# A decoder trunk's first microseconds: gain row fetched first on ScalarE's queue, first two weight units in pieces, rotary angles on GpSimd

## The chip, the cores and the metric

The kernel runs on one core of one Trainium2 chip. The metric is device time in microseconds (us) of one execution, lower is better, as the median of several runs. A core has TensorE (PE, matmuls and transposes), VectorE (DVE), ScalarE (ACT), GpSimd (POOL) and SyncE (SP, which only issues DMAs here). ScalarE and GpSimd also issue DMAs from their own queues.

## What is computed

Two decoder layers on 256 tokens of width 1024 in float32. Layer 0 mixes tokens by sliding-window attention with rotary positions, layer 1 by a gated delta rule. Each layer has two feed-forward blocks around the mixer:

```python
x = x + 0.5 * rmsnorm(swiglu(rmsnorm(x, norms[0]), w_in[0], w_out[0]), norms[1])
x = x + rmsnorm(mixer(rmsnorm(x, norms[2])), norms[3])
x = x + 0.5 * rmsnorm(swiglu(rmsnorm(x, norms[4]), w_in[1], w_out[1]), norms[5])

def swiglu(x, w_in, w_out):
    gate, up = jnp.split(x @ w_in, 2, axis=-1)
    return (jax.nn.silu(gate) * up) @ w_out

def rope_tables(positions, head_dim):
    ...
    ang = positions.astype(jnp.float32)[..., None] * inv_freq
    return jnp.cos(ang), jnp.sin(ang)
```

The hidden width of a feed-forward block is 2816. The rotary angles are 256 positions times 8 frequencies; they are used first in the attention of layer 0, which is the second of six stages.

## The kernel before

All matrix products are split: each float32 operand becomes a high part in the format fp32r (ScalarE copies it) and a low part (VectorE subtracts the high part from the original), and TensorE makes three products, high by high, weights' low by high, and weights' high by low. The weights of a stage come in **units** of 128 partitions x 2048 columns, 1 MB, through three slots of `w_raw`, each with its pair in `w_high` and `w_low`. SP issues a unit as two DMAs of 512 KB, and the fourth unit and all later ones wait until `w_lo` says that the low part of the unit three before is made (L284). ScalarE's `hi` makes the high part (L571, in the loop L577), VectorE's `lo` the low part (L1322).

The stages are ffn, swa, ffn, ffn, gdn, ffn. A feed-forward stage runs over 11 steps of 256 hidden columns; one step takes two units of `w_in` (four of the eight 128-row blocks of x each) and one of `w_out`. Each engine has its program written out by hand, in order, and steps 1 to 9 of a feed-forward stage are a hardware loop on each engine.

The start of the first stage (`enter(0)` on ScalarE and VectorE, `begin` and `first_tile` on TensorE) is what the change touches. Rows of x come in two tiles of 128 tokens, `t` = 0 and 1. VectorE multiplies each tile by the norm's weight row, in two halves of 512 columns (`x_gained`, L1394); the row, replicated over 128 partitions, is `gain_rows`, loaded by GpSimd's `gain_load` (L347). TensorE transposes each half (L855), and four **quarters** m = 0 to 3 of x turned stand in PSUM banks 6 and 7: ScalarE makes their high part (`turned`, L587), VectorE their low part (L1329). TensorE's first weight products (L844 to L846) are those of unit 0 with tile 0; then come the first half of unit 1, the transposes of quarter 2, the second half of unit 1 and the transposes of quarter 3, the last ones (`first_tile`). The norm's factor is not needed for that: it scales the products afterwards (`rstd`, from sums of squares of x by ScalarE, L621, and VectorE, L1420, and a power by GpSimd, L386 and L387), ahead of SiLU (L634).

After that VectorE runs `mul(0)`, `lo` of units 3 and 4, and `angles` (L1342 to L1364, the function of that name), once per launch; then its loop begins with the low part of the turned hidden units (`turn`, L1437), whose high part is ScalarE's (L639). TensorE's first product of `w_out` (L875) waits for it. The angles are reduced to the range of the sine; ScalarE computes sine and cosine from them after its loop of the first stage. GpSimd meanwhile loads the next gain rows and forms wide products for the next norm (`base_of_next`, L517 and L520).

The small constants (positions, sinks, decay parameters, convolution weights) are loaded by the first five instructions of ScalarE; two larger ones follow after the high part of unit 1 (L580, L581).

Of the kernel before, what the change touches and what calls it, by code (L numbers as in the profile page):

```python
# [34 lines left out]
P = 128  # L35
D = 1024
KT = D // P
TT = 2
# [46 lines left out]
def build(nc, x, positions, l0_norms, l0_ffn_w_in, l0_ffn_w_out, a_w_in, a_b_in, a_sinks, a_w_out,  # L85
# [4 lines left out]
    with ExitStack() as ctx:  # L90
# [72 lines left out]
        cwr = view(10752, P)  # L163

# [29 lines left out]
        raw_in = [sem(f"raw_in{s}") for s in range(SLOTS)]  # L194
        gain_in = [sem(f"gain_in{s}") for s in range(2)]
        w_hi, w_lo, w_used = sem("w_hi"), sem("w_lo"), sem("w_used")
        ident_built, tables = sem("ident_built"), sem("tables_built")
# [8 lines left out]
        trig, dve_trig, cw_ps, cw_done = sem("trig"), sem("angles"), sem("conv_w_psum"), sem("conv_w")  # L206
# [71 lines left out]
        def _(sp):  # L278
# [24 lines left out]

            def ffn(base, wi, wo):
                slot(base, 0, up(wi, 0, 0))
                if base == 0:
                    sp.dma_start(xs[:, 1, :], x[0, P:S, :]).then_inc(x_in[1], 16)
                slot(base + 1, 1, up(wi, 0, 4))
# [33 lines left out]
        def _(pool):  # L342
# [10 lines left out]
            gain_load(0)  # L353
# [26 lines left out]
            last.then_inc(tables, 1)  # L380
            gain_load(1)

# [128 lines left out]
            def base_of_next(n, kind):  # L511

                if kind == "gdn":
                    pool.wait_ge(c3["r1"], NG)
                pool.wait_ge(gain_in[0], 16 * (n + 2))
# [39 lines left out]
        def _(act):  # L555
            act.dma_start(posi[:], positions.rearrange("a (t p) -> p (a t)", p=P),
                          allow_slow_non_contiguous=True).then_inc(const_in, 16)
            act.dma_start(sink[:], a_sinks.partition_broadcast(P)).then_inc(const_in, 16)
            act.dma_start(alog[:], b_A_log.partition_broadcast(P)).then_inc(const_in, 16)
            act.dma_start(dtb[:], b_dt_bias.partition_broadcast(P)).then_inc(const_in, 16)  # L560
            act.dma_start(cwr[0:TAPS * CT, :], b_conv_w.rearrange("t (c p) -> (t c) p", p=P)).then_inc(const_in, 16)
# [17 lines left out]
            def large_constants():  # L579
                act.dma_start(bias, a_b_in.partition_broadcast(P)).then_inc(const_in, 16)  # L580
                act.dma_start(nrm[:], b_norm.partition_broadcast(P)).then_inc(const_in, 16)  # L581
# [13 lines left out]

            def enter(n):
# [20 lines left out]
                if n:  # L617
                    act.wait_ge(x_new[0], n)
                else:
                    act.wait_ge(x_in[0], 16)  # L620
                act.activation(junk[:, 0, :], xs[:, 0, :], ACT.Square, accum_out=xss[:, 0:1]).then_inc(xsq[0], 1)  # L621

            def ffn(n):
# [27 lines left out]
                if n == 0:  # L651
                    act.wait_ge(dve_trig, 1)
# [188 lines left out]
        def _(pe):  # L841
# [42 lines left out]
            def begin(n):  # L884

                ti = TBASE[n]
                if n == 0:
                    turn_x(ti, 0)
                turn_x(ti, 1)
                pe.wait_ge(w_lo, UBASE[n] + 1)  # L890
                pe.wait_ge(xT_lo, 4 * ti + 1)
# [6 lines left out]
            def ffn(n):  # L898
# [36 lines left out]
                def first_tile():  # L935

                    up(0, 0, 0)
                    pe.wait_ge(w_lo, base + 2)
# [375 lines left out]
        def _(dve):  # L1314
# [23 lines left out]
            def angles():  # L1338

                dve.wait_ge(const_in, 16 * 7)  # L1340
                dve.wait_ge(tables, 1)
                dve.tensor_scalar(nsink[:], sink[:], -1.0, None, ALU.mult)  # L1342
                link(dve.tensor_copy(ang[:, 2, 0:TT], posi[:]))
                for t in range(TT):
                    last = dve.tensor_scalar(ang[:, 3, t * HALF:(t + 1) * HALF], es[:, 0, 0:HALF], ang[:, 2, t:t + 1], None,
                                             ALU.mult)
                link(last)
                magic = 1.5 * 2.0 ** 23
                c1 = 6.28125
                c2 = float(np.float32(TWO_PI - c1).view(np.uint32).__and__(np.uint32(0xfffff000)).view(np.float32))  # L1350
                c3_ = TWO_PI - c1 - c2
                turns = ang[:, 2, :]
                for i, quarter in enumerate((0.0, 0.25)):
                    r = ang[:, i, :]
                    link(dve.tensor_scalar(turns, ang[:, 3, :], 1.0 / TWO_PI, quarter, ALU.mult, ALU.add))
                    link(dve.tensor_scalar(turns, turns, magic, None, ALU.add))
                    link(dve.tensor_scalar(turns, turns, magic, None, ALU.subtract))
                    src = ang[:, 3, :]
                    for part in (c1, c2, c3_):
                        link(dve.scalar_tensor_tensor(out=r, in0=turns, scalar=-part, in1=src, op0=ALU.mult, op1=ALU.add))  # L1360
                        src = r
                    if quarter:
                        link(dve.tensor_scalar(r, r, TWO_PI / 4, None, ALU.add))
                    ins = dve.tensor_scalar(r, r, PI_BELOW, -PI_BELOW, ALU.min, ALU.max)  # L1364
                    if i == 0:
                        link(ins)
                ins.then_inc(dve_trig, 1)
# [12 lines left out]
            def enter(n):  # L1380
# [7 lines left out]
                else:  # L1388
                    dve.wait_ge(gain_in[0], 16)
                    for t in range(TT):  # L1390
# [5 lines left out]
                        if t == 0:  # L1396
                            turned(ti, 0)
                            lo(0, 0)
                            turned(ti, 1)
                    lo(1, 1)  # L1400
# [23 lines left out]
            def ffn(n):  # L1424
# [18 lines left out]
                if n == 0:  # L1443
                    angles()
# [280 lines left out]
```

## Time and profile before

| | |
|---|---|
| median of 3 runs | 1157.38 us (1157.25 to 1158.41) |
| span of the profiled execution | 1156.0 us |
| TensorE busy | 1084.4 us, 94% |
| VectorE, ScalarE, GpSimd busy | 668.9, 502.9 and 215.7 us |
| bytes moved | 178.62 MB, 155 GB/s on average |
| first stage (ffn) | the first 211 us or so |

The span runs from the first to the last instruction of one profiled execution; the time of a run lies 1.4 us above it. A busy TensorE is not TensorE at its peak: its clock is granted in two levels, and the profile shows which. In a timeline a row gives the start, the length, the engine and the line, what is written and read, how many instructions are merged in the row, and in square brackets how long the engine had been idle before it and what ended that. A line such as L844 can belong to many instructions.

### The profile page before, as it was taken

Reading aid. Unit: us, or ns where it says so; the run is one execution under the profiler, and the core shown is the slowest. Engines: PE = TensorE matmul, PEld = TensorE weight load, DVE = VectorE, ACT = ScalarE, POOL = GpSimd, SP = SyncE. Lnnn points to the kernel's source line nnn. Section 1 sums busy time; section 2 is a strip of 40 time slices with the busy share of each in tenths; the row PEclk is TensorE's granted clock in tenths of the full one; section 3 lists DMA queues with packets and bytes.
Section 4 is the critical chain, followed back from the end, with each engine's and each line's share of the span. In section 5 each row is a group of like instructions: output and inputs, shape, how many; then the busy total and the mean of one; then the engine's idle time right before and its main releaser. Section 6 shows DMA issues by size and latency. Waiting matters only on the chain.

```text
span 1156.0 us, 14795 instructions
## 1 busy us (share of the span) xinstructions
PE 1084.4 (94%) x5403; PEld 901.1 (78%) x5403; DVE 668.9 (58%) x708; ACT 502.9 (44%) x608; POOL 215.7 (19%) x261
## 2 busy tenths in 40 slices
PE   4799999889989999998999998999999988999997
PEld 3688888667768888877888886778889966888885
DVE  3844554756576445557555547786674568554454
ACT  2444444444354444444434444784632235444442
POOL 4300000260243000005100002244244343000000
PEclk9899999989999999999999999998999999999999
DMA  8556555351047565545655562643410014755640
GB/s 281 165 180 199 181 188 195 110 218 37 3 142 257 182 197 182 200 148 192 208 181 182 185 205 84 222 156 133 146 38 1 1 48 131 239 182 181 195 169 36
DMA packets 124631, 178.62 MB, mean 155 GB/s; under 512 B 7248, under 2 KB 98608, under 8 KB 124592
## 3 DMA queue, kind: packets, MB, share of 16 engines
q1 hardware_dynamic: 121760, 171.00, 44.8%
q0 software_dynamic: 1728, 6.29, 1.5%
q10 hardware_dynamic: 1104, 0.79, 0.2%
q8 instruction: 26, 0.43, 0.1%
q14 instruction: 13, 0.11, 0.0%
HBM read 177.01 MB, written 1.05 MB: 154 GB/s over the span
## 4 chain that ended last, share of the span: by engine, by line
PE 78%; DVE 11%; POOL 4%; ACT 3%; issue 2%; DMA 2%; DVEq 0%; POOLq 0%; SPq 0%; ACTq 0%
PE banks L844 15%; PE banks L846 14%; PE banks L845 14%; PE banks L875 7%; PE banks L877 7%; PE banks L880 7%; PE banks L1117 6%; DVE w_low L1322 3%; DVE x_gained L1378 2%; PE banks L908 2%; ACT w_high L571 1%; DVE mixer_arena L1334 1%; PE banks L1086 1%; ACT squares L593 1%; POOL pow_base L386 1%
## 5 line engine op out<-in xcount | busy, mean ns | idle before, releaser
L1322 DVE TENSOR_TENSOR w_low<-w_raw,w_high 128x2048 fp32r<-128x2048 f32 x162 | 379.8, 2348 | 224.1 <-ACT w_high L577 182.3
L844 PE MATMUL banks<-w_high,xT_high 128*128 128x512 f32 (+1 forms) x880 | 352.1, 400 | 11.6 <-DVE w_low L1322 5.1
L846 PE MATMUL banks<-w_high,xT_low 128*128 128x512 f32 (+1 forms) x880 | 344.7, 392 | 0.0
L845 PE MATMUL banks<-w_low,xT_high 128*128 128x512 f32 (+1 forms) x880 | 344.2, 391 | 0.0
L577 ACT ACTIVATE w_high<-w_raw 128x2048 fp32r<-128x2048 f32 x108 | 206.4, 1911 | 122.4 <-PE banks L880 120.9
L844 PEld LDWEIGHTS banks<-w_high,xT_high 128*128 128x128 f32 x880 | 167.4, 190 | 48.2 <-DVE w_low L1322 9.2
L846 PEld LDWEIGHTS banks<-w_high,xT_low 128*128 128x128 f32 x880 | 167.0, 190 | 35.4
L845 PEld LDWEIGHTS banks<-w_low,xT_high 128*128 128x128 f32 x880 | 167.7, 191 | 32.1
L386 POOL TENSOR_SCALAR pow_base<-y_sumsq 128x1 f32<-128x1 f32 x12 | 5.9, 493 | 678.7 <-ACT squares L593 678.7
L875 PE MATMUL banks<-w_high,hT_high 128*128 128x512 f32 x320 | 125.9, 393 | 7.1 <-DVE hT_low L1437 7.1
L877 PE MATMUL banks<-w_low,hT_high 128*128 128x512 f32 x320 | 125.3, 391 | 0.0
L571 ACT ACTIVATE w_high<-w_raw 128x2048 fp32r<-128x2048 f32 x54 | 102.9, 1914 | 25.0 <-PE banks L846 10.9
L880 PE MATMUL banks<-w_high,hT_low 128*128 128x512 f32 x320 | 99.1, 391 | 0.0
L634 ACT ACTIVATE mixer_arena<-banks,rstd 128x256 f32<-128x256 f32 x88 | 41.4, 475 | 113.9 <-PE banks L846 104.3
L639 ACT ACTIVATE hT_high<-banks 128x512 fp32r<-128x512 f32 x40 | 23.9, 599 | 146.6 <-PE banks L908 146.6
L1117 PE MATMUL banks<-mixer_arena 128*128 128x128 f32 x688 | 79.4, 276 | 1.2 <-DVE mixer_arena L1625 0.8
L1117 PEld LDWEIGHTS banks<-mixer_arena 128*128 128x128 f32 x688 | 77.9, 192 | 2.0 <-DVE mixer_arena L1625 1.0
L875 PEld LDWEIGHTS banks<-w_high,hT_high 128*128 128x128 f32 x320 | 60.6, 189 | 19.9 <-issue 7.5
L1437 DVE TENSOR_TENSOR hT_low<-banks,hT_high 128x512 fp32r<-128x512 f32 x40 | 27.7, 691 | 80.2 <-ACT hT_high L639 80.2
L880 PEld LDWEIGHTS banks<-w_high,hT_low 128*128 128x128 f32 x320 | 60.4, 189 | 12.6
L877 PEld LDWEIGHTS banks<-w_low,hT_high 128*128 128x128 f32 x320 | 60.6, 189 | 12.3
L1430 DVE SCALAR_TENSOR_TENSOR mixer_arena<-banks,rstd,mixer_arena 128x256 f32<-128x256 f32 x88 | 41.9, 481 | 39.5 <-ACT mixer_arena L634 39.5
(211 smaller groups left out, 1008.9 us busy)
## 6 DMA issues: line engine op xcount, KB each, us to landing
w_raw<-in_l_ffn_w_in SPq DMA_DIRECT2D x176, 512.0 KB, 4.7
w_raw<-in_l_ffn_w_out SPq DMA_DIRECT2D x88, 512.0 KB, 4.0
w_raw<-in_b_w_in SPq DMA_DIRECT2D x32, 512.0 KB, 4.5
gain_rows<-in_l_norms POOLq DMA_DIRECT2D x12, 512.0 KB, 7.2
w_raw<-in_a_w_in SPq DMA_DIRECT2D x10, 512.0 KB, 4.2
w_raw<-in_a_w_out SPq DMA_DIRECT2D x8, 512.0 KB, 6.4
w_raw<-in_b_w_out SPq DMA_DIRECT2D x8, 512.0 KB, 3.7
x_rows<-in_x SPq DMA_DIRECT2D x2, 512.0 KB, 7.6
```

The costliest lines, as they stand in the source:

```text
L571: act.activation(whi[:, c % 3, 0:n], raw[:, c % 3, 0:n], ACT.Copy).then_inc(w_hi, 1)
L577: act.activation(whi[:, c % 3, :], raw[:, c % 3, :], ACT.Copy).then_inc(w_hi, 1)
L634: act.activation(sg[:, t, :], PS[:, banks[t], 0:FC], ACT.Silu, scale=rstd[:, t:t + 1]).then_inc(silu_done, 1)
L844: pe.matmul(dst, sh, wh, start=start, stop=False)
L845: pe.matmul(dst, sh, wl, start=False, stop=False)
L846: return pe.matmul(dst, sl, wh, start=False, stop=stop)
L875: pe.matmul(PS[:, 2 * t + h, :], sh[:, k, tok], whi[:, c % 3, cols], start=start and k == 0, stop=False)
L877: pe.matmul(PS[:, 2 * t + h, :], sh[:, k, tok], wlo[:, c % 3, cols], start=False, stop=False)
L880: last = pe.matmul(PS[:, 2 * t + h, :], sl[:, k, tok], whi[:, c % 3, cols], start=False, stop=stop and k == 1)
L1117: last = pe.matmul(PS[:, bank, col(i)], lhs(i), rhs(i), start=start, stop=True)
L1322: dve.tensor_tensor(wlo[:, c % 3, :], raw[:, c % 3, :], whi[:, c % 3, :], ALU.subtract).then_inc(w_lo, 1)
L1430: dve.scalar_tensor_tensor(out=gated[:, t, :], in0=PS[:, banks[t], FC:2 * FC], scalar=rstd[:, t:t + 1], in1=sg[:, t, :], op0=ALU.mult, op1 ...
```

## The change

- ScalarE's first instruction is now the DMA of the first gain row, on its own queue, with the semaphore `gain_first`. GpSimd no longer loads it, and its waits for gain rows count one less.
- SP issues unit 0 as four DMAs of 256 KB (one block of 128 rows of `w_in` each), then unit 1 in the same way, and the second tile of x only after them. Before, that tile stood between unit 0 and unit 1.
- ScalarE and VectorE split unit 0 in four pieces of 512 columns and unit 1 in two of 1024, between the quarters of x. TensorE waits for the pieces one by one.
- ScalarE squares the first tile of x behind these pieces instead of at the end of `enter(0)`; all seven constants are loaded after that.
- The angles are computed by GpSimd, after the norm's factor and two more gain loads and ahead of `base_of_next`. Each SCALAR_TENSOR_TENSOR (multiply and add) of VectorE becomes two instructions on GpSimd, through a scratch view `cwr_free`.

On SP, the beginning of the program before (`x_rows` is x, `w_raw` the weights' slots):

```order
L315 DMA x_rows<-in_x 128x1024
L284 DMA w_raw<-in_l_ffn_w_in 128x4x256 x2
L307 DMA x_rows<-in_x 128x1024
L284 DMA w_raw<-in_l_ffn_w_in 128x4x256 x2
L309 UNCONDITIONAL_BRANCH
```

and with the change:

```order
L334 DMA x_rows<-in_x 128x1024
L315 DMA w_raw<-in_l_ffn_w_in 128x2x256 x4
L318 DMA w_raw<-in_l_ffn_w_in 128x2x256 x4
L320 DMA x_rows<-in_x 128x1024
L328 UNCONDITIONAL_BRANCH
```

The second tile of x went from the fourth place to the tenth.

On VectorE, from the first instruction to the first of its loop, before (`x_gained` is x times the gain row, `xT_low` the low part of x turned, `hT_low` that of the hidden units):

```order
L1394 TENSOR_TENSOR x_gained<-x_rows,gain_rows 128x512 x2
L1329 TENSOR_TENSOR xT_low<-banks,xT_high 128x4x128
L1322 TENSOR_TENSOR w_low<-w_raw,w_high 128x2048
L1329 TENSOR_TENSOR xT_low<-banks,xT_high 128x4x128
L1394 TENSOR_TENSOR x_gained<-x_rows,gain_rows 128x512 x2
L1322 TENSOR_TENSOR w_low<-w_raw,w_high 128x2048
...
L1322 TENSOR_TENSOR w_low<-w_raw,w_high 128x2048 x2
L1342 TENSOR_SCALAR minus_sinks<-sinks 128x16
...
L1364 TENSOR_SCALAR mixer_arena<-mixer_arena 128x16
L1445 UNCONDITIONAL_BRANCH
L1437 TENSOR_TENSOR hT_low<-banks,hT_high 128x512
```

and with the change:

```order
L1476 TENSOR_TENSOR x_gained<-x_rows,gain_rows 128x512 x2
L1438 TENSOR_TENSOR w_low<-w_raw,w_high 128x512
L1422 TENSOR_TENSOR xT_low<-banks,xT_high 128x4x128
L1438 TENSOR_TENSOR w_low<-w_raw,w_high 128x512 x2
L1422 TENSOR_TENSOR xT_low<-banks,xT_high 128x4x128
L1438 TENSOR_TENSOR w_low<-w_raw,w_high 128x512
L1448 TENSOR_TENSOR w_low<-w_raw,w_high 128x1024
L1476 TENSOR_TENSOR x_gained<-x_rows,gain_rows 128x512 x2
L1448 TENSOR_TENSOR w_low<-w_raw,w_high 128x1024
...
L1415 TENSOR_TENSOR w_low<-w_raw,w_high 128x2048 x2
L1529 UNCONDITIONAL_BRANCH
L1523 TENSOR_TENSOR hT_low<-banks,hT_high 128x512
```

The angles stand no longer between the splits of units 3 and 4 and the low part of the hidden units, and the second tile of x has one weight piece behind it.

The diff, cut to its core:

```diff
         def _(sp):
+            def first_units(w):
+                v = w.rearrange("(k p) (s n) -> p k s n", p=P, s=2)
+                r = [raw[:, c, :].rearrange("p (k s n) -> p k s n", k=4, s=2) for c in range(2)]
+                for k in range(4):
+                    sp.dma_start(r[0][:, k, :, :], v[:, k, :, 0:FC]).then_inc(
+                        first_in[k] if k < 2 else raw_in[0], 16)
+                for k in range(4):
+                    sp.dma_start(r[1][:, k, :, :], v[:, 4 + k, :, 0:FC]).then_inc(
+                        second_in if k < 2 else raw_in[1], 16)
+                sp.dma_start(xs[:, 1, :], x[0, P:S, :]).then_inc(x_in[1], 16)
...
         def _(pool):
-            gain_load(0)
...
+            def angles():
+                pool.wait_ge(const_in, 16 * 7)
+                pool.tensor_scalar(nsink[:], sink[:], -1.0, None, ALU.mult)
...
+                    for part in (c1, c2, c3_):
+                        link(pool.tensor_scalar(step, turns, -part, None, ALU.mult))
+                        link(pool.tensor_tensor(r, step, src, ALU.add))
...
                     gain_load(2 * n + 2)
+                if n == 0:
+                    angles()
...
         def _(act):
+            act.dma_start(gain[:, 0, :], l0_norms[0].partition_broadcast(P)).then_inc(gain_first, 16)
...
                 else:
+                    first_piece(0)
                     turned(ti, 0)
+                    first_piece(1)
+                    first_piece(2)
                     turned(ti, 1)
-                    hi(0, 0)
-                    hi(1, 1)
-                    large_constants()
+                    first_piece(3)
+                    second_piece(0)
+                    second_piece(1)
+                    square_x(n)
+                    constants()
                 turned(ti, 2)
                 turned(ti, 3)
...
         def _(pe):
...
+                        for k in range(4):
+                            if k < 3:
+                                pe.wait_ge(first_lo, k + 1)
+                            else:
+                                pe.wait_ge(w_lo, 1)
+                            wide(0, 0, PS[:, 4, :], 512, 4, 0, True, False, (k,))
+                        pe.wait_ge(second_lo, 1)
                     pe.wait_ge(xT_lo, 4 * ti + 2)
                     wide(1, 0, PS[:, 4, :], 512, 4, 4, False, False, (0, 1))
                     turn_x(ti, 2)
+                    if n == 0:
+                        pe.wait_ge(w_lo, 2)
...
         def _(dve):
-                    dve.wait_ge(gain_in[0], 16)
+                    dve.wait_ge(gain_first, 16)
...
                 lo(base + 4, 4)
-                if n == 0:
-                    angles()
```

## Rows read from the trace of the kernel before

**Rows 1.** The page's head: the span of the profiled execution.

```profile
span 1156.0 us, 14795 instructions
```

**Rows 2.** Chain of waits, 0 to 20 us: start, length in us, what.

```profile
1.31 8.67 DMA gain_rows<-in_l_norms
...
10.01 0.70 DVE x_gained L1394
...
10.84 1.96 PE banks L855 x8
...
13.42 1.80 ACT w_high L571
...
15.25 2.30 DVE w_low L1322
```

**Rows 3.** Timeline of TensorE, 17 to 51 us, four rows.

```profile
17.59 0.80 PE L844 MATMUL banks<-w_high,xT_high 128*128 128x512 f32 x1 [4.81 <-DVE w_low L1322]
...
26.40 0.60 PE L855 MATMUL banks<-ident,x_gained 128*128 128x128 f32 x4
...
43.46 0.39 PE L846 MATMUL banks<-w_high,xT_low 128*128 128x512 f32 x1
50.91 0.77 PE L875 MATMUL banks<-w_high,hT_high 128*128 128x512 f32 x1 [7.06 <-DVE hT_low L1437]
```

**Rows 4.** Timeline of ScalarE (ACTq: its DMA issues), 11 to 39 us.

```profile
11.97 0.60 ACT L587 ACTIVATE xT_high<-banks 128x512 fp32r<-128x512 f32 x1 [7.12 <-PE banks L855]
...
16.55 1.91 ACT L571 ACTIVATE w_high<-w_raw 128x2048 fp32r<-128x2048 f32 x1 [1.34 <-DMA w_raw<-in_l_ffn_w_in]
16.56 0.35 ACTq L580 DMA_DIRECT2D mixer_arena<-in_a_b_in  x1
...
38.39 0.60 ACT L639 ACTIVATE hT_high<-banks 128x512 fp32r<-128x512 f32 x1 [1.28 <-PE banks L908]
```

**Rows 5.** Timeline of VectorE, 18 to 51 us, and one split near 361 us.

```profile
18.06 1.28 DVE L1394 TENSOR_TENSOR x_gained<-x_rows,gain_rows 128x512 f32<-128x512 f32 x2
...
35.34 4.49 DVE L1322 TENSOR_TENSOR w_low<-w_raw,w_high 128x2048 fp32r<-128x2048 f32 x2 [1.29 <-ACT w_high L571]
...
40.03 4.80 DVE L1345 TENSOR_SCALAR mixer_arena<-exp_sink,mixer_arena 128x8 f32<-128x8 f32 x2
...
50.07 0.69 DVE L1437 TENSOR_TENSOR hT_low<-banks,hT_high 128x512 fp32r<-128x512 f32 x1
...
361.26 3.03 DVE L1322 TENSOR_TENSOR w_low<-w_raw,w_high 128x2048 fp32r<-128x2048 f32 x1 [1.38 <-ACT w_high L577]
```

**Rows 6.** Stretches (us): length, PE, PEld, DVE, ACT, POOL busy, clock, DMA share, GB/s.

```profile
50.90:54.20 3.30, 3.29 (x8) 2.63 (x9) 3.30 (x4) 0.00 (x0) 0.00 (x0) 0.50 0.00 0
54.30:200.00 145.70, 145.70 (x661) 120.66 (x661) 72.22 (x51) 60.22 (x53) 0.00 (x0) 1.00 0.58 191
340.00:380.00 40.00, 39.93 (x181) 32.74 (x180) 25.08 (x17) 19.25 (x17) 13.56 (x7) 1.00 0.71 236
```

**Rows 7.** Timeline of GpSimd, 30 to 47 us, near 239 us and near 355 us.

```profile
30.57 1.25 POOL L386 TENSOR_SCALAR pow_base<-x_sumsq 128x2 f32<-128x2 f32 x1 [14.68 <-ACT squares L621]
...
40.06 2.40 POOL L517 TENSOR_TENSOR mixer_arena<-gain_rows 128x1024 f32<-128x1024 f32 x1 [6.51 <-DMA gain_rows<-in_l_norms]
42.43 4.67 POOL L520 TENSOR_TENSOR x_gained<-x_rows,gain_rows 128x1024 f32<-128x1024 f32 x2
...
239.16 0.22 POOL L401 TENSOR_TENSOR mixer_arena<-mixer_arena,cos_rows 128x16 f32<-128x16 f32 x1
...
355.33 6.81 POOL L520 TENSOR_TENSOR x_gained<-x_rows,gain_rows 128x1024 f32<-128x1024 f32 x2
```

**Rows 8.** DMA, 0 to 20 us: ScalarE's queue q10; issues, KB each, us to landing.

```profile
q10 hardware_dynamic: 848, 0.23, 6.4%
...
x_rows<-in_x SPq DMA_DIRECT2D x1, 512.0 KB, 4.0
...
mixer_arena<-in_a_b_in ACTq DMA_DIRECT2D x1, 640.0 KB, 5.7
```

More of the change, by code:

```diff
@@ L194, in build @@
         raw_in = [sem(f"raw_in{s}") for s in range(SLOTS)]
+        gain_first = sem("gain_first")
         gain_in = [sem(f"gain_in{s}") for s in range(2)]
         w_hi, w_lo, w_used = sem("w_hi"), sem("w_lo"), sem("w_used")
-        ident_built, tables = sem("ident_built"), sem("tables_built")
+        first_in = [sem(f"first_in{k}") for k in range(2)]
+        second_in = sem("second_in")
+        first_hi, first_lo, second_hi, second_lo = (
+            sem("first_hi"), sem("first_lo"), sem("second_hi"), sem("second_lo"))
+        ident_built = sem("ident_built")
         xg_ready, xT_ps, xT_hi, xT_lo = sem("xg_ready"), sem("xT_psum"), sem("xT_hi"), sem("xT_lo")
@@ L205, in build @@
         dve_own, pool_own = sem("dve_own"), sem("pool_own")
-        trig, dve_trig, cw_ps, cw_done = sem("trig"), sem("angles"), sem("conv_w_psum"), sem("conv_w")
+        trig, angle_done, cw_ps, cw_done = sem("trig"), sem("angles"), sem("conv_w_psum"), sem("conv_w")
         sp_ready, qkv_ready, rope_ready = sem("swa_proj"), sem("qkv_ready"), sem("rope_ready")
@@ L379, in _ @@
                 last = pool.memset(es[:, 0, i:i + 1], float(freq[i]))
-            last.then_inc(tables, 1)
+            link(last)
             gain_load(1)
+            def angles():
+                pool.wait_ge(const_in, 16 * 7)
+                pool.tensor_scalar(nsink[:], sink[:], -1.0, None, ALU.mult)
+                link(pool.tensor_copy(ang[:, 2, 0:TT], posi[:]))
+                for t in range(TT):
+                    last = pool.tensor_scalar(ang[:, 3, t * HALF:(t + 1) * HALF], es[:, 0, 0:HALF],
+                                              ang[:, 2, t:t + 1], None, ALU.mult)
+                link(last)
+                magic = 1.5 * 2.0 ** 23
+                c1 = 6.28125
+                c2 = float(np.float32(TWO_PI - c1).view(np.uint32).__and__(np.uint32(0xfffff000)).view(np.float32))
+                c3_ = TWO_PI - c1 - c2
+                turns, step = ang[:, 2, :], cwr_free
+                for i, quarter in enumerate((0.0, 0.25)):
+                    r = ang[:, i, :]
+                    link(pool.tensor_scalar(turns, ang[:, 3, :], 1.0 / TWO_PI, quarter, ALU.mult, ALU.add))
+                    link(pool.tensor_scalar(turns, turns, magic, None, ALU.add))
+                    link(pool.tensor_scalar(turns, turns, magic, None, ALU.subtract))
+                    src = ang[:, 3, :]
+                    for part in (c1, c2, c3_):
+                        link(pool.tensor_scalar(step, turns, -part, None, ALU.mult))
+                        link(pool.tensor_tensor(r, step, src, ALU.add))
+                        src = r
+                    if quarter:
+                        link(pool.tensor_scalar(r, r, TWO_PI / 4, None, ALU.add))
+                    ins = pool.tensor_scalar(r, r, PI_BELOW, -PI_BELOW, ALU.min, ALU.max)
+                    if i == 0:
+                        link(ins)
+                ins.then_inc(angle_done, 1)
             def power(out, src, scale, shift, n, final=None):
@@ L594, in square_y, with first_piece, second_piece, square_x @@
                                ACT.Square, accum_out=yss[:, t:t + 1]).then_inc(ysq, 1)
+            def first_piece(k):
+                if k < 2:
+                    act.wait_ge(first_in[k], 16)
+                else:
+                    act.wait_ge(raw_in[0], 32)
+                at = slice(k * 512, k * 512 + 512)
+                act.activation(whi[:, 0, at], raw[:, 0, at], ACT.Copy).then_inc(first_hi if k < 3 else w_hi, 1)
+            def second_piece(i):
+                if i:
+                    act.wait_ge(raw_in[1], 32)
+                else:
+                    act.wait_ge(second_in, 32)
+                at = slice(i * 1024, i * 1024 + 1024)
+                act.activation(whi[:, 1, at], raw[:, 1, at], ACT.Copy).then_inc(w_hi if i else second_hi, 1)
+            def square_x(n):
+                if n:
+                    act.wait_ge(x_new[0], n)
+                else:
+                    act.wait_ge(x_in[0], 16)
+                act.activation(junk[:, 0, :], xs[:, 0, :], ACT.Square, accum_out=xss[:, 0:1]).then_inc(xsq[0], 1)
             def enter(n):
@@ L1336, in scaled @@
                             wait=False)
[L1338 to L1367, printed above, removed]
@@ new lines, in first_piece, with second_piece @@
+            def first_piece(k):
+                if k < 3:
+                    dve.wait_ge(first_hi, k + 1)
+                else:
+                    dve.wait_ge(w_hi, 1)
+                at = slice(k * 512, k * 512 + 512)
+                dve.tensor_tensor(wlo[:, 0, at], raw[:, 0, at], whi[:, 0, at], ALU.subtract
+                                  ).then_inc(first_lo if k < 3 else w_lo, 1)
+            def second_piece(i):
+                if i:
+                    dve.wait_ge(w_hi, 2)
+                else:
+                    dve.wait_ge(second_hi, 1)
+                at = slice(i * 1024, i * 1024 + 1024)
+                dve.tensor_tensor(wlo[:, 1, at], raw[:, 1, at], whi[:, 1, at], ALU.subtract
+                                  ).then_inc(w_lo if i else second_lo, 1)
```

49 lines of the change are left out of this document (28 added, 21 removed).

## The prediction

> **What bounds the kernel now.** I read the page first: TensorE is busy for nearly the whole span of 1156.0 us [rows 1]. A kernel of that kind gets shorter by what TensorE spends idle or at its low clock, so I looked for those places near the code that the change touches. There are three, all in the first 55 us.
>
> The first is the wait ahead of the first weight product. The chain of waits [rows 2] is one line: the gain row, fetched from GpSimd's queue, takes 8.67 us and lands at 9.98; VectorE multiplies it into x (0.70 a half); TensorE turns both halves of x (1.96); ScalarE takes the high part of x, then of the whole weight unit 0 (1.80 on the chain); VectorE makes the low part (2.30); only then, at 17.59, does TensorE start on weights [rows 3].
>
> The second is the low clock after that start. The third is a hole: TensorE's last product of step 0 starts at 43.46 and the next one at 50.91, after 7.06 us of idleness put down to VectorE's low part of the turned hidden units [rows 3]. ScalarE had given the high part by 38.39 + 0.60 = 38.99 [rows 4]. VectorE was done with its two splits at 35.34 + 4.49 = 39.83, but then computed the rotary angles until 50.07 [rows 5]. The clock shows in the stretches [rows 6]: idle at 43.9 to 50.9, TensorE is granted 0.50 (1.2 GHz) for the next 3.3 us, then 1.00 (2.4 GHz) up to 200 us.
>
> **Part 1: the angles leave VectorE.** Without them the low part starts at 39.83 and takes 0.69 [rows 5], so it is there at 40.52, 3.3 us before TensorE asks for it (43.86, the row at 43.46 with its 0.39). The hole of 7.06 us goes entirely. With it goes the slow restart: 3.3 us at half speed did the work of 1.65 us, so 1.65 us more. Sum: **8.7 us**. Late next would be the following split (2.3 us, started at 40.52 and done near 42.9), which TensorE needs only after a further 24 products, near 49.3.
>
> On GpSimd the angles are 25 instructions, since each fused multiply-add becomes two. A small GpSimd product takes 0.22 us [rows 7]; with its own semaphore wait I count 0.27, so 25 x 0.27 = 6.8 us undisturbed. But they meet VectorE's splits. Two rows show what such a meeting costs: GpSimd's 128x2 TENSOR_SCALAR at 30.57 took 1.25 us instead of a fifth of that, ending where a split of VectorE ended [rows 7]; and the two 128x8 TENSOR_SCALARs of the angles took 4.80 us on VectorE [rows 5] while GpSimd made its wide products (2.40 and 4.67, from 40.06) [rows 7]. So I bound the 25 from below by 6.8 and from above by 25 x 2.3 = 58 us, and take about 15, as only some five or six splits fall in that time. ScalarE asks for the angles after the loop of the first stage, near 185 us. Even 58 us are covered; without that cover the sine, and the step behind it, would wait. The Trainium skill, page "SBUF — State Buffer", section "SBUF: two separate sides", says that a VectorE instruction with two SBUF inputs and a GpSimd instruction that reads SBUF exclude each other for a whole instruction. By that rule, the trace agrees (4.80 and 1.25 us above), and the rule speaks against the move: the angles can now block splits that they only preceded before.
>
> What does a blocked split cost? One small GpSimd instruction holds it for 0.2 to 0.3 us. The three wide products behind the angles hold one for up to 2.4 us each. The nearest case is the third stage: the wide products run there from about 352 to 362 us (6.81 for the last two) [rows 7], a split of 2.3 us is stretched to 3.03 [rows 5], and TensorE is still busy 39.93 of 40 us [rows 6]. I take **0**, and keep 3 us for the range.
>
> **Part 2: the gain row comes first, on ScalarE's queue.** Its price is not in the trace, so I bound it. The same 512 KB, x's first rows on SP's hardware queue, took 4.0 us from an issue at 0.81 [rows 8]. A broadcast row of 640 KB on ScalarE's queue, under full weight traffic, took 5.7 [rows 8]. Issued at 0.81 it lands between 4.8 and 6.5, at worst as before, 9.98 less the 0.5 that its issue is earlier. I take 6.2: it shares the engines with x. The first piece of weights (256 KB, right behind x) should be there near 7.
>
> **Part 3: unit 0 in four pieces.** After the gain row: one half of x 0.70, four transposes 1.1 (10.84 to 11.97, [rows 2, 4]), the high part 0.60 [rows 4], the low part 0.69 [rows 5], and some 0.3 of handing over: 3.4 us. A piece of 512 columns needs a quarter of 1.9 and 2.3 us and is done beside that. So the first weight product starts at 6.2 + 3.4 = **9.6** instead of 17.59. That alone is 8.0 us, but it isn't kept: what counts is when the last transpose of x's second half is done, since from there on both programs are alike. Before, this is 26.40 + 0.60 = 27.0, which is 9.4 after the first weight product with every operand at hand [rows 3]. TensorE alone would so allow 9.6 + 9.4 = 19.0.
>
> **Part 4: x's second half now comes behind both weight units.** VectorE's queue has it ahead of the last weight piece. In bytes it stands where the second half of unit 1 stood: ScalarE waited for that until 16.55 [rows 4]. The small constants no longer go first; their queue used 6.4% of the sixteen engines over 20 us, or 1.3 us of all of them [rows 8], so x's second half lands near 15.3. Behind it: two halves of x 1.28 [rows 5], half a split 1.15, six products and four transposes 2.1 (with the transposes 0.60, [rows 3]): 4.5 us, so **19.8**. This is later than 19.0, and it decides. Gain over before: 27.0 - 19.8 = **7.2 us**. Bounds: if it lands at 13.5, TensorE decides at 18 to 19 (8 to 9 us); if it lands at 16.55 and TensorE has dropped to its low clock meanwhile, 22.3 (4.7 us).
>
> **Part 5: the rest.** Seven DMA issues (0.35 to 0.5 us each, [rows 4]), some 3.3 us, now stand on ScalarE between the square of x and the high part of x's second half. The square starts near 14.9 when the pieces are through, and issues ran beside an ACTIVATE before (16.56 in the row at 16.55), so they end near 18.3, about when the first transposed quarter is ready: **0**, with 1 us for the range. The square of x moves ahead, but GpSimd's first step for the norm ended with VectorE's split and not with the square, so that wins nothing. GpSimd's first DMA is gone, and its masks start 0.7 us earlier: nobody waits. The constants land by about 28 us, where GpSimd comes to the angles; SP's queue has nine transfers ahead of unit 2 instead of five, with the same bytes.
>
> **Sum:** 7.2 + 8.7 = 15.9 us. The profiled span of 1156.0 becomes 1140.1; the median is 1.4 us above the span, so **1141.5 us**.
>
> **The rivals.** (a) *The forecast*, 1139.5 to 1143.5: chance 0.62. (b) *Late data*: x's second half or the pieces land so late that the first part brings 3 to 5 us: 1143.7 to 1145.7. For it speaks that each of the first transfers took far longer than its bytes; against, that the constants are out of the way. 0.13. (c) *The queue is not the reason*: the gain row lands near 9.5 on ScalarE's queue too. Then the first weight product is at 12.9 and the quarter at 12.9 + 9.4 = 22.3, a gain of 4.7 and a time of 1157.4 - 4.7 - 8.7 = 1144.0. Against it stands the 4.0 us of x. 0.08. The Trainium skill, page "DMA: Bandwidth & Descriptors", section "Anatomy of one DMA — SWDGE (gpsimd) path", gives about 2.0 us + bytes/436e3 for such a transfer, and its table puts the hardware path only 0.4 us ahead; by it this rival would be right. The row of 8.67 us for 512 KB, against an estimate of 3.2 us from that page, does not agree. (d) *GpSimd blocks the splits*: three wide products hold up three splits for 2.4 us each; 7.2 less the 3.3 us of slack leaves 3.9 us of hole: 1145.4, or 1147 if the clock falls again. The third stage speaks against. 0.07. (e) *Better*: the data is there before TensorE and the clock rises sooner: 1137.5 to 1139.5. 0.07. (f) *Slower*: the scattered start (transposes, pieces, waits between) keeps TensorE at 1.2 GHz. Each us at half speed loses 0.5, so the 15.9 us are used up only after 32 us more at the low clock than before, and at 40 us the time is 1157.4 + 4 = 1161. Against it: before, the clock rose within 6 us of the first weight product, with an emptier start ahead of it. 0.03.
>
> **How the numbers follow.** Cases (a) to (d) are all faster. A measurement of this kernel tells about 0.2% (2.3 us) from no change, and only (f) lies outside; I give "within 0.2%" 0.02 for a mixture of (b), (d) and (f). The range leaves out (f), half of (e) and the end of (d): 1138.5 to 1146.5.
>
> **What would show it.** In the changed profile: the gain row landing at 5 to 6.5; the first weight product near 9.6; x's second half near 15.3, with VectorE waiting for it; the last transpose of x near 19.8; no idleness of TensorE over 1 us between there and 60 us, and a clock of 1.00 all along; 25 small instructions on GpSimd from about 28 us, some of 2.3 us; and the sine on ScalarE without a wait. A gain row at 9 or later, a hole behind it, or a wait for x over 2 us would make the prediction wrong.

## The result and the profile after

The changed kernel takes **1139.31 us** (median of 4 runs, 1138.89 to 1140.52) against 1157.34 before (4 runs): 18.0 us less, a ratio of 0.9843 with a 95% interval of 0.9829 to 0.9857. Forecast were 1141.5 us and a gain of 15.9. The profiled execution:

```profile
span 1137.1 us, 14812 instructions
```

The chain of waits of the changed kernel from its start, to be read beside [rows 2] (start, length in us, what):

```profile
0.80 5.41 DMA gain_rows<-in_l_norms
6.24 0.70 DVE x_gained L1476
7.07 1.10 PE banks L936 x4
8.20 0.61 ACT xT_high L640
8.83 0.70 DVE xT_low L1422
9.57 0.80 PE banks L925
```

The gain row lands at 6.21 instead of 9.98, no split of a whole unit stands in the chain any more, and the first weight product starts at 9.57 instead of 17.59. The timeline of TensorE (last column: idleness before the row and what ended it) shows the transposes of x and the first product of `w_out`, beside [rows 3]:

```profile
7.07 1.94 PE L936 MATMUL banks<-ident,x_gained 128*128 128x128 f32 x8 [7.07 <-DVE x_gained L1476]
9.57 0.80 PE L925 MATMUL banks<-w_high,xT_high 128*128 128x512 f32 x1 [0.56 <-DVE xT_low L1422]
...
18.09 0.60 PE L936 MATMUL banks<-ident,x_gained 128*128 128x128 f32 x4
...
35.38 0.39 PE L956 MATMUL banks<-w_high,hT_high 128*128 128x512 f32 x1
```

The last transpose of x ends at 18.69 instead of 27.0, and the first product of `w_out` at 35.38 has no bracket: TensorE did not wait. The stretches of the changed kernel (length; PE, PEld, DVE, ACT, POOL busy; clock; DMA share; GB/s) say the same of what follows, where before there was the hole and then a clock of 0.50 [rows 6]:

```profile
20.00:55.00 35.00, 35.00 (x160) 28.97 (x159) 22.52 (x19) 19.22 (x17) 26.57 (x31) 1.00 0.77 262
```

VectorE's timeline, to compare with [rows 5], has the one wait for x's second half, and the low part of the hidden units right behind two splits:

```profile
13.69 1.33 DVE L1476 TENSOR_TENSOR x_gained<-x_rows,gain_rows 128x512 f32<-128x512 f32 x2 [0.49 <-DMA x_rows<-in_x]
14.95 1.25 DVE L1448 TENSOR_TENSOR w_low<-w_raw,w_high 128x1024 fp32r<-128x1024 f32 x1
...
27.04 4.50 DVE L1415 TENSOR_TENSOR w_low<-w_raw,w_high 128x2048 fp32r<-128x2048 f32 x2 [1.29 <-ACT w_high L617]
31.46 0.68 DVE L1523 TENSOR_TENSOR hT_low<-banks,hT_high 128x512 fp32r<-128x512 f32 x1
...
42.97 2.66 DVE L1415 TENSOR_TENSOR w_low<-w_raw,w_high 128x2048 fp32r<-128x2048 f32 x1 [1.76 <-ACT w_high L623]
```

The two splits that met GpSimd's wide products behind the angles are the longest ones here, 2.66 us and

```profile
49.33 3.07 DVE L1415 TENSOR_TENSOR w_low<-w_raw,w_high 128x2048 fp32r<-128x2048 f32 x1 [1.11 <-ACT w_high L623]
```

against 2.3 undisturbed; TensorE did not wait for either. On GpSimd, beside [rows 7], the angles run from 25.29 to 39.07; most of the 25 instructions take 0.2 to 0.3 us, and three are stretched:

```profile
25.29 0.30 POOL L404 TENSOR_SCALAR minus_sinks<-sinks 128x16 f32<-128x16 f32 x1
...
27.18 2.27 POOL L419 TENSOR_SCALAR mixer_arena<-mixer_arena 128x16 f32<-128x16 f32 x1
29.53 2.12 POOL L422 TENSOR_SCALAR mixer_arena<-mixer_arena 128x16 f32<-128x16 f32 x1
...
39.03 4.45 POOL L566 TENSOR_TENSOR mixer_arena<-gain_rows 128x1024 f32<-128x1024 f32 x1
43.45 6.80 POOL L569 TENSOR_TENSOR x_gained<-x_rows,gain_rows 128x1024 f32<-128x1024 f32 x2
```

**Where the 18.9 us between the two spans are.** GpSimd's first step for the norm at the start of the second stage is a milestone in both traces, 230.88 before and 213.71 after:

```profile
230.88 2.09 POOL L386 TENSOR_SCALAR pow_base<-x_sumsq 128x2 f32<-128x2 f32 x1 [5.57 <-DVE x_sumsq L1420]
```
```profile
213.71 2.10 POOL L435 TENSOR_SCALAR pow_base<-x_sumsq 128x2 f32<-128x2 f32 x1 [5.57 <-DVE x_sumsq L1506]
```

So 17.2 us come from the first stage: 8.3 from the start (27.0 to 18.69), 7.1 from the hole, 1.6 from the slow restart, 0.2 unassigned. The other 1.7 us come from the second stage (109.19 before, 108.42 after, from milestone to milestone) and the fifth (247.75, 246.81), whose work did not change. The third and fourth differ by less than 0.1 us.

### The profile page after: what moved, and what is told of

Read it like the earlier page. It is cut to its first block, busy times and chain, and to the rows that moved or that the text cites. A ratio compares the mean times of both kernels' runs of the same rounds, so it can differ in the third digit from the quotient of the medians.

```text
span 1137.1 us, 14812 instructions
## 1 busy us (share of the span) xinstructions
PE 1080.0 (95%) x5403; PEld 897.1 (79%) x5403; DVE 661.2 (58%) x693; ACT 503.8 (44%) x612; POOL 233.5 (21%) x285
## 4 chain that ended last, share of the span: by engine, by line
PE 80%; DVE 10%; POOL 4%; ACT 3%; issue 2%; DMA 1%; DVEq 0%; POOLq 0%; SPq 0%; ACTq 0%
PE banks L925 15%; PE banks L927 15%; PE banks L926 15%; PE banks L956 7%; PE banks L961 7%; PE banks L958 7%; PE banks L1210 6%; DVE w_low L1415 2%; DVE x_gained L1460 2%; PE banks L990 2%; DVE mixer_arena L1427 1%; PE banks L1179 1%; ACT squares L646 1%; ACT w_high L617 1%; POOL pow_base L435 1%
## 5 line engine op out<-in xcount | busy, mean ns | idle before, releaser
L623 ACT ACTIVATE w_high<-w_raw 128x2048 fp32r<-128x2048 f32 x108 | 206.4, 1911 | 113.4 <-PE banks L961 111.2
L617 ACT ACTIVATE w_high<-w_raw 128x2048 fp32r<-128x2048 f32 x52 | 99.1, 1914 | 24.6 <-PE banks L927 11.0
```

The lines of the kernel that those rows point to most:

```text
L617: act.activation(whi[:, c % 3, 0:n], raw[:, c % 3, 0:n], ACT.Copy).then_inc(w_hi, 1)
L623: act.activation(whi[:, c % 3, :], raw[:, c % 3, :], ACT.Copy).then_inc(w_hi, 1)
```

## The experiments

Differences to the kernel before are against its runs on the same chip (medians 1157.58 for the first four experiments, 1156.70 for the next four, 1156.49 for the last four). The change itself was timed beside runs with a median of 1157.34, so a difference "to the change" compares medians of different groups and is uncertain by up to 0.9 us; where it matters, the milestone of the second stage decides.

**The two parts apart.** `e1_angles_only` is the kernel before with the angles written for GpSimd as in the change: called there behind the gain loads, and no longer on VectorE.

```diff
                 lo(base + 4, 4)
-                if n == 0:
-                    angles()
...
                     gain_load(2 * n + 2)
+                if n == 0:
+                    angles()
```

> The kernel before with one part of the change: the angles are computed by GpSimd, the start is as before. Theory (the two parts add up): the hole of 7.06 us ahead of the first product of w_out and the 3.3 us at 1.2 GHz behind it go, 8.7 us, so 1148.6 us. Rival (GpSimd's 25 instructions and three wide products hold up VectorE's splits): 3 to 4 us of the hole stay, 1152 us.

Measured: 1146.99 us, 10.6 less (ratio 0.9904, interval 0.9888 to 0.9921). TensorE no longer waits behind step 0; the milestone at the second stage moves by 9.1 us (221.82), as expected with a gain row that landed 0.3 us earlier; the rest came later, in stages with the same code. `e2_start_only` is the changed kernel with the angles back on VectorE.

> The changed kernel with the angles back on VectorE, behind the splits of units 3 and 4; the start is as in the change. Theory (the parts add up): 8.3 us faster than before from the start alone, 1149.0 us, with a hole of about 7 us behind step 0. Rival (what was gained at the start is partly taken back by the hole, since the constants and the gain row for GpSimd's wide products come later relative to it): a hole of 8 us or more, 1151 us.

Measured: 1149.96 us, 7.6 less (0.9929, 0.9913 to 0.9946). The start is that of the change, and the hole is the old one:

```profile
9.58 0.79 PE L892 MATMUL banks<-w_high,xT_high 128*128 128x512 f32 x1 [0.56 <-DVE xT_low L1389]
...
42.80 0.77 PE L923 MATMUL banks<-w_high,hT_high 128*128 128x512 f32 x1 [6.89 <-DVE hT_low L1521]
```

10.6 and 7.6 make 18.2, the change gave 18.0; at the milestone 9.1 and 7.9 make 17.0 of 17.2. The parts add up, and neither rival holds.

**Is it the queue?** `e3_gain_queue_only` puts the gain row first on ScalarE's queue in the kernel before, with the constants behind it.

```diff
-            gain_load(0)
...
+            act.dma_start(gain[:, 0, :], l0_norms[0].partition_broadcast(P)).then_inc(gain_first, 16)
```

> The kernel before with the first gain row issued by ScalarE as its first instruction, the small constants behind it, nothing else. Theory (hardware queue and place in it decide): the row lands at 5 to 6.5 us instead of 9.98, but the second half of unit 0 lands only at 12 or so, after which come 1.9 and 2.3 us of splitting: first weight product at 16.4, 1 us gained, 1156.3 us. Rival (the queue is not the reason, the row lands near 9.5): 0.5 us or nothing, 1157 us, with the row's landing as the difference.

Measured: 1154.74 us (median of 10 runs, 1154.03 to 1157.37), 2.8 less by the medians and 2.3 by the ratio (0.9980, 0.9970 to 0.9989), where 1 us was expected. The row lands at 6.1, the whole unit 0 at 11.23, and the first weight product starts at 15.52 instead of 17.59; the milestone comes 2.6 us earlier. `e4_gain_on_gpsimd` is the other way round: the change, with that row as GpSimd's first instruction again.

```diff
-            act.dma_start(gain[:, 0, :], l0_norms[0].partition_broadcast(P)).then_inc(gain_first, 16)
...
+            pool.dma_start(gain[:, 0, :], l0_norms[0].partition_broadcast(P)).then_inc(gain_first, 16)
```

> The changed kernel with the first gain row issued by GpSimd as its first instruction; all else as changed. Theory A (the software queue is slow): the row lands at 9 to 9.5, first weight product near 12.7, 3 us slower than the change, 1142.4 us. Theory B (what stood ahead and beside it, the small constants and the weights in large pieces, was slow): the row lands near 6.7, 0.5 us slower than the change, 1139.8 us.

Measured: 1142.87 us, 3.6 more than the change (0.9873, 0.9857 to 0.9890, against before). VectorE's first row there, and the DMA row (KB, us to landing):

```profile
8.68 1.34 DVE L1476 TENSOR_TENSOR x_gained<-x_rows,gain_rows 128x512 f32<-128x512 f32 x2 [8.68 <-DMA gain_rows<-in_l_norms]
```
```profile
gain_rows<-in_l_norms POOLq DMA_DIRECT2D x1, 512.0 KB, 7.3
```

With the constants out of the way and the weights in pieces, GpSimd's queue still needs 7.3 us where ScalarE's needs 5.4. Theory A holds, in a smaller size: the first weight product comes at 12.02, the last transpose ends at 20.43 instead of 18.69, and the milestone is 1.7 us later than the change's (215.45). Only these 1.7 of the 3.6 us belong to the edit; in the profile the second and the fifth stage, with the same code, were longer by 1.2 and 1.6 us.

**How slow are the angles by themselves?** `e5_wide_after_angles` is the kernel before with one wait more.

```diff
+                if n == 0:
+                    pool.wait_ge(dve_trig, 1)
                 pool.wait_ge(gain_in[0], 16 * (n + 2))
```

> The kernel before with one wait more: GpSimd starts its three wide products for the next norm only when VectorE's angles are done. The angles stay on VectorE. Theory (much of the hole was GpSimd holding up the angles, three of whose instructions took 7.07 us instead of 0.5): the angles end near 43.5, TensorE waits 0.5 us instead of 7.06 and keeps its clock, 8.2 us gained, 1149.3 us. Rival (the angles are slow in themselves): the hole stays at 6 us or more, 1157 us.

Measured: 1150.25 us, 6.5 less (0.9942, 0.9926 to 0.9959). On VectorE the instructions that took 4.80 [rows 5] are now a row of 0.37, and TensorE's hole is 0.54:

```profile
39.84 0.37 DVE L1347 TENSOR_SCALAR mixer_arena<-exp_sink,mixer_arena 128x8 f32<-128x8 f32 x2
...
43.35 0.69 DVE L1439 TENSOR_TENSOR hT_low<-banks,hT_high 128x512 fp32r<-128x512 f32 x1
```
```profile
44.19 0.47 PE L877 MATMUL banks<-w_high,hT_high 128*128 128x512 f32 x1 [0.54 <-DVE hT_low L1439]
```

At the second stage's milestone this single wait is worth 8.2 us of the 9.1 that the move of the angles brings (8.8 of them without the earlier gain row). The wide products of GpSimd had made the hole, not the angles' own 3.7 us. The meeting is only put off: right behind, a split takes 4.02 us and the last two wide products 8.86 instead of 4.67, but there TensorE does not wait for them.

**Constants, pieces, order of x.** `e6_constants_early` issues the five small constants directly behind the gain row in the changed kernel.

> The changed kernel with the five small constants issued directly behind the gain row on ScalarE's queue, as early as before. Theory (they slow the first transfers): x's second half lands at 15 instead of 13.69 and decides, 0.8 us slower than the change, 1140.3 us. Rival (they cost nothing, TensorE decides either way): 1139.5 us, x's second half within 0.3 us of 13.69.

Measured: 1141.30 us (1139.85 to 1143.12), 2.0 more than the change, 1.3 of it at the milestone (215.01). The theory holds: x's second half lands at 15.34 instead of 13.69 (13.63 to 13.69 in the five profiles with the change's order of loads); TensorE waits for pieces of weights three times (0.23, 0.32 and 0.84 us) and ends the last transpose at 19.98. `e7_whole_units` is the change without pieces, here on ScalarE, and on SP, VectorE and TensorE alike.

```diff
-                    first_piece(0)
                     turned(ti, 0)
-                    first_piece(1)
-                    first_piece(2)
                     turned(ti, 1)
-                    first_piece(3)
-                    second_piece(0)
-                    second_piece(1)
+                    hi(0, 0)
+                    hi(1, 1)
```

> The changed kernel without the pieces: units 0 and 1 are loaded as two DMAs each and split whole (high part 1.9 us, low part 2.3 us), as before; gain row, order of x, constants and angles as changed. Theory (pieces are needed for the early row to count): unit 0 is complete near 10.2, first weight product at 14.5, last transpose of x 9.1 us later at 23.6 instead of 18.7, 4.9 us slower than the change, 1144.3 us. Rival (x's second half decides, not the first weight product): within 1.5 us of the change, 1140.8 us.

Measured: 1143.93 us, 4.6 more than the change, 4.4 of it at the milestone (218.09); first weight product at 13.89, last transpose at 23.07. The pieces are needed, as the theory said. `e8_x_between` puts x's second half back between the units.

> The changed kernel with x's second half issued between the pieces of unit 0 and those of unit 1, its old place. Theory A (x's second half decides the last transpose): it lands near 10.5 and the last transpose comes up to 1 us earlier, 1138.4 us. Theory B (TensorE alone decides, as its unbroken row of products from 9.57 says): no difference, 1139.4 us, last transpose at 18.1 still.

Measured: 1142.01 us, but from 1139.42 to 1142.46, 2.7 more by the median. Only 0.6 us of it belong to the edit (milestone of the second stage at 214.28 instead of 213.71: the last piece of unit 1 now makes TensorE wait 0.24 us, and the last transpose ends at 19.24). The remainder lies in the second and fifth stage again. Neither theory was right: an earlier x only makes the last weights later.

**The clock.** The leftover 1.7 us led to holes that the change does not touch. In the attention stage TensorE waits 5.13 us for GpSimd and restarts at 1.2 GHz. The stretches behind that wait, before, after, and in the kernel with the gain row on GpSimd's queue:

```profile
250.80:253.80 3.00, 3.00 (x12) 2.71 (x13) 0.00 (x0) 1.63 (x3) 0.00 (x0) 0.50 0.97 319
253.80:256.80 3.00, 3.00 (x10) 2.12 (x8) 0.00 (x0) 0.85 (x1) 0.00 (x0) 0.70 0.06 22
```
```profile
233.60:236.60 3.00, 3.00 (x11) 2.75 (x12) 0.00 (x0) 1.58 (x3) 0.00 (x0) 0.50 1.01 320
236.60:239.60 3.00, 3.00 (x18) 2.07 (x16) 0.63 (x1) 0.90 (x1) 0.00 (x0) 0.98 0.07 23
```
```profile
235.30:238.30 3.00, 2.98 (x11) 2.76 (x12) 0.00 (x0) 1.55 (x3) 0.00 (x0) 0.50 1.01 308
238.30:241.30 3.00, 3.00 (x9) 2.31 (x8) 0.00 (x0) 0.93 (x1) 0.00 (x0) 0.54 0.08 28
```

The same instructions after the same wait get the high clock back after about 5, 3 and 6 us. `e11_fill_attention_hole` keeps TensorE busy in that hole; for that, one of its two waits moves ahead of the transposes:

```diff
+                        pe.wait_ge(qkv_ready, 2)
+                        for _ in range(40):
+                            pe.transpose(PS[:, 5, 0:P], ident[:], ident[:])
                         pe.wait_ge(rope_ready, 4)
-                        pe.wait_ge(qkv_ready, 2)
```

> The changed kernel with 40 transposes of the identity on TensorE in the attention stage, where it waits 5.1 us for GpSimd's rotary products. Theory (the part of the gain over the sum of the start and the hole, and the spread between runs, is this hole's restart at 1.2 GHz, whose length differs): the granted clock stays 1.00 there, and from the second scaling of the first stage to that of the second it takes 107.0 us instead of 108.4 to 109.7; 1.4 us or more gained, 1138.0 us. Rival (the clock isn't the cause): within 108.4 to 109.7 as in the others, 1139.4 us.

The stretch behind the wait is then

```profile
233.30:236.30 3.00, 2.91 (x17) 2.57 (x18) 0.00 (x0) 2.20 (x3) 0.04 (x1) 1.00 0.99 310
```

and the second stage takes 106.92 us from milestone to milestone, against 108.23 to 109.73 in the twelve profiles without it. Theory confirmed for that stage. The other profiles say the same: in stretches of half a us, TensorE's busy time at a granted clock of 0.50 in this stage adds up to 2.9 us where the stage was shortest (108.23), 3.1 in the change (108.42), 4.9 before (109.19), 6.1 where it was longest (109.73), and 0 with the filling; half of that is close to the excess over 106.92 (in the change 1.6 and 1.5 us). The time is 1138.55 us (1136.84 to 1139.01), only 0.8 less than the change, and within the uncertainty between the groups: in its profile the fifth stage, with holes of its own, took 248.69 us, the longest seen.

`e9_warm` puts 20 such transposes at TensorE's very start.

> The changed kernel with 20 more 128x128 transposes of the identity on TensorE right at its start (into a PSUM bank not yet in use), before the first transposes of x. Theory: they raise the clock ahead of the weight products, which then take 0.23 us each instead of 0.43; the last transpose of x is bound by VectorE's last piece of unit 1 (done at 16.2) and comes at 18.3 instead of 18.7: 0.4 us gained, 1139.0 us, with small waits of TensorE for pieces from 10 to 16 us. Rival: short transposes don't raise the clock, products at 0.43 as before, 1139.4 us.

They do raise the clock (the eight transposes of x take 1.30 us instead of 1.94, the products behind are 0.23 apart), and TensorE waits for data instead:

```profile
1.79 4.05 PE L1403 MATMUL banks<-ident 128*128 128x128 f32 x20 [1.79 <-POOL ident L375]
7.03 1.30 PE L936 MATMUL banks<-ident,x_gained 128*128 128x128 f32 x8 [1.20 <-DVE x_gained L1478]
9.10 0.50 PE L925 MATMUL banks<-w_high,xT_high 128*128 128x512 f32 x1 [0.77 <-DVE xT_low L1424]
...
16.25 0.50 PE L925 MATMUL banks<-w_high,xT_high 128*128 128x512 f32 x1 [0.90 <-DVE w_low L1450]
```

The last transpose ends at 18.34 and the milestone is 0.36 us earlier, as expected; the time, 1139.74 us (1139.43 to 1141.03), cannot show so little. With x's second half ahead of the last two pieces of unit 1 as well, nothing more is gained:

> As the kernel with 20 transposes more at the start, and x's second half issued ahead of the last two pieces of unit 1. Theory: both land by 13.7, VectorE has nothing to wait for in between, last transpose near 18.0, 1138.7 us. Rival (what bounds is when the last of the 3.7 MB lands and VectorE's work behind it): same as without the new order within 0.3 us.

Measured: 1139.66 us, 0.1 from the kernel with the old order, as the rival said; last transpose at 18.09, but then a wait of 0.31 us for its low part, and a milestone of 213.72, that of the change.

`e12_warm_and_fill` has both sets of transposes.

> The changed kernel with both sets of transposes, 20 at the start and 40 in the attention stage's hole. Theory: both gains add up, 0.4 + 1.4 us: 1137.6 us. Rival: neither raises or keeps the clock, 1139.4 us.

Measured: **1135.83 us** (median of 5, 1134.73 to 1136.92), ratio 0.9812 to the kernel before, interval 0.9799 to 0.9826. That is 3.5 us below the change by the medians and 2.6 if each is taken against its own runs of the kernel before; the lowest run of the change (1138.89) lies above the highest one here, and it is the fastest of all kernels here. Between the two profiled executions lie 2.0 us (1137.1 and 1135.1), and their milestones place them: 0.4 in the first stage, 1.5 in the second (106.93), 0.15 in the fifth (246.66). That is the expected sum of 0.4 and 1.4 us. The rest of the difference of the medians is between runs without a profile: the profiled run of the change is the fastest of its four, the one here the slowest of its five. The mean granted clock of the run fits that (0.993 in the profiled run, 0.996 to 0.997 in the four others, 0.990 to 0.994 in the change's), but which stages had it, no trace shows.

The 0.4 us at the start do not need the high clock from the first weight product on. Here the clock fell again just ahead of it: it is 0.50 from 9 to 12 us, the first products are 0.43 apart as in the change, and the pace rises at 12.2 (in the change at 14.8). Still the last transpose ends at 18.34, as with the 20 transposes alone, since TensorE waits for VectorE's last piece in either case:

```profile
9.07 0.79 PE L925 MATMUL banks<-w_high,xT_high 128*128 128x512 f32 x1 [0.77 <-DVE xT_low L1426]
...
16.23 0.50 PE L925 MATMUL banks<-w_high,xT_high 128*128 128x512 f32 x1 [0.78 <-DVE w_low L1452]
```

## Why the prediction was right, and where it was not

- **The hole goes entirely, 8.7 us: right.** No wait, and a clock of 1.00 to 55 us. That nothing late took its place was read from the 3.3 us between 40.52 and 43.86; after the change the low part is ready at 32.14 and asked for at about 35.4.
- **GpSimd's angles cost nothing: right.** 13.7 us instead of 15, three meetings with splits instead of five or six. The wide products stretched two splits, to 2.66 and 3.07 us, and TensorE never waited between the last transpose and 60 us: rival (d) is out.
- **Gain row at 6.2, first weight product at 9.6: right** (6.21 and 9.57). Rival (c), that the queue is not the reason, is refuted by the run with GpSimd's queue: 8.68 and 12.02, 1.7 us at the milestone. The prediction let this rival rest on the Trainium skill, page "DMA: Bandwidth & Descriptors": a fit in the section "Anatomy of one DMA — SWDGE (gpsimd) path", and 0.4 us between the paths, which stand in its section "Specifications" and are counted to the first byte. No run here shows the first byte. Up to the landing, beside the weights' stream, the rows have 1.9 us (7.3 and 5.4), and 0.5 us more in the issue, so 0.4 us is not what the move from one queue to the other is worth here.
- **x's second half near 15.3 and deciding: wrong in size, and so in what decides.** It landed at 13.69. The term that was mis-sized is what the small constants and the gain row cost the other transfers: counted were 1.3 us, from the share of the constants' queue. The constants alone are 1.65 (15.34 against 13.69, with and without them early), and the gain row on GpSimd's queue another 1.0 (whole units landed at 15.54 instead of 16.55 when that row moved to the head of ScalarE's queue, the constants 0.4 us later behind it): together 2.65 of the 2.86 us from 16.55 to 13.69. Then TensorE alone decides, as the unused bound of 19.0 said; it ended at 18.69, since the clock rose some 5.2 us after the first product instead of 5.7. That moment is not fixed: with the same start it came after 6.2 us in `e2_start_only`, and the last transpose ended at 19.09. Gain 8.3 instead of 7.2.
- **It was rival (e) that came true, not (a).** "The data is there before TensorE and the clock rises sooner", 1137.5 to 1139.5, had a chance of 0.07; the 1139.31 us lie in it, just below the forecast's 1139.5, and so does what happened at the start. But the start gave only 1.1 us more than forecast. With the 1.7 us of the later stages, which no part of the sum foresaw, left out, the profiled span would be 1138.8 us (forecast: 1140.1) and the time 1140.6 to 1141.0, inside (a): that it ended in (e)'s interval is in good part luck.
- **The hole's cause was named only in part.** The prediction had the 4.80 us row as evidence of a lock between VectorE and GpSimd, but did not draw that the hole was mostly this lock. One wait on GpSimd removes 8.2 us. The form that the prediction names for the lock, a VectorE instruction with two SBUF inputs, also fits only its 1.25 us row, where a split ran beside; the TENSOR_SCALARs of the 4.80 us row read one tensor and one value per partition, the next one (44.86, 2.27 us instead of 0.17) one tensor and constants, and they were held all the same.
- **Left out: the restarts behind other holes.** The sum treated all later stages as equal. The later stages gave 1.7 us of the 18.9 between the profiled spans. Over the twelve profiles without the filling the second stage varies by 1.5 us, and over all fourteen the fifth varies by 2.0. For the attention hole the run with the filling, and the low-clock time of all profiles, show that it is the clock. For the fifth stage the clock is not enough: TensorE's busy time at 0.50 there is 6.8 us in the change (246.81), but 9.9 in the shortest (246.66) and 10.1 in the longest (248.69). One wait of TensorE in it, for VectorE's `gdn_small`, also differs (2.1, 1.4 and 2.5 us in these three). Why is open.

## What to carry to other kernels

When a row of tiny instructions takes microseconds, look at what GpSimd reads at that moment before moving the work: postponing GpSimd's wide products by one wait gave nearly all of what moving the work gave (8.2 of 9.1 us at the milestone; 6.5 and 10.6 in the total, which carries the later stages). At a kernel's start put first, on a hardware queue, the one transfer at which the chain of waits begins, keep tiny transfers behind the large ones, and split the first operands so that TensorE starts on a quarter. And read a gain from milestones inside the trace as well as from the total: here the total carries up to 3 us that belong to later stages with unchanged code, in the second of them to the clock's restart.

## What was not expected of the hardware

- A 512 KB broadcast from GpSimd's queue takes 7.3 to 8.7 us at the start of the program and 5.4 on ScalarE's.
- Five transfers of 1 to 48 KB, 65 KB in all, on ScalarE's queue delay the end of a stream of 3.1 MB on another queue by 1.65 us.
- An equal wait of 5.1 us is followed by 3 to 6 us at 1.2 GHz, differently in kernels that have the same code there; 128x128 transposes are enough to raise the clock, and 40 of them kept it through that wait. The 20 at the start kept it up to the weight products in two kernels, but not in the third (`e12_warm_and_fill`), with the same TensorE program up to there.
- Ahead of its first change the record of the granted clock is no guide: it shows 1.00 where products are 0.43 us apart.

```profile
9.57:14.80 5.23, 5.23 (x12) 4.13 (x13) 4.74 (x7) 4.47 (x7) 4.57 (x11) 1.00 1.08 364
```

Twelve products in 5.23 us are 0.43 us apart, the pace that other rows show at a granted clock of 0.50; at 1.00 they are 0.23 apart.
